# A decoder layer with PEER experts on one Trainium2 core: three steps of the query projection stage put in other places

## The chip, the cores and the metric

The kernel runs on one core of one Trainium2 chip. The metric is the device time in microseconds (us) of one execution. Its engines are TensorE (PE, with its weight loads as PEld), VectorE (DVE), ScalarE (ACT), GpSimd (POOL) and SyncE (SP); each works through its own instructions in order and waits on semaphores where the program says so. In this kernel SyncE issues the loads of the dense weights, and GpSimd issues the loads of `w_ada` and all gathers of expert rows.

## The reference

One layer on a sequence of 256 tokens, width 2048, all float32. A conditioning vector gives six vectors through `w_ada` (shift, scale, gate, twice); attention (two kinds, 8 heads each) with its output projection gives `x`; then comes the expert mixer, which is where the change lies:

```python
h2 = rmsnorm(x, norm2_g[l]) * (1.0 + sc2) + sh2
x = x + g2 * peer_ffn(h2, w_peer_q[l], peer_keys1[l], peer_keys2[l], peer_u[l], peer_v[l])
# peer_ffn, for each token and each of 8 heads:
q = h2 @ w_q                      # 8 heads x 2 halves x 128
v1, i1 = top_k(q[..., 0, :] @ keys1.T, 16); v2, i2 = top_k(q[..., 1, :] @ keys2.T, 16)
best, pos = top_k(v1[:, None] + v2[None, :], 16)      # expert = i1 * 128 + i2
gates = softmax(best)
act = gelu(u_tab[expert] @ h2)                        # one dot of 2048 for each of 16 experts
y += (gates * act) @ v_tab[expert]                    # rows of 2048
```

The result is normed once more. With 256 tokens, 8 heads and 16 experts that makes 32,768 rows of `peer_u` and as many of `peer_v`, 8 KB each.

## The kernel before

The tokens are two tiles of 128 (one per partition). The first half millisecond holds the adaLN sums, the input projection, attention and the output projection; this text is about what comes after them.

**Jobs and slots.** A job `q` is one head of one token tile, 16 jobs in all. A slot `n` (0 to 255) is one expert place of one job, `n = 16 q + k`. For a slot, one gather fetches 128 rows of `peer_u` into `u_rows` (7 buffers) and one fetches 128 rows of `peer_v` into `v_rows` (9 buffers).

**GpSimd** (L1130 to L1170) issues all gathers in one fixed order. `gather_u(n)` waits for the experts of its job, and from n = 7 on for the dot of slot n - 7, whose buffer it takes. Slot 6 takes the buffer in which an adaLN sum lay and so waits until `ada_cols(5)` has read it (`ada_columns`, L1148). The v-gathers trail: v-gather 0 stands right behind u-gather 24, v-gather 1 behind u-gather 25 and so on. v-gather 0 waits for projection `p5`, v-gather 4 for `p7`, the last, since the buffers lie in the ring of dense weights.

**VectorE** (`serve`, L1605) does for each slot `dot(n)`, a multiply of 128 x 2048 with the sum over the row written to `hidden`, and then a few pieces of `retrieve`, the top-16 search of a later job. Once per job it does `weights(q - 1)`: it waits for ScalarE's `exponent(q - 1)` and `gelu(q - 1)` and writes gate times activation into `hidden`.

**ScalarE** moves projections, scores and token rows out of PSUM, does `exponent(q)` (softmax numerator) and `gelu(q)` (which waits for the 16 dots of job q), and builds for each slot a diagonal matrix `diag` out of the weight of each token.

**TensorE** first does the eight query projections `p0` to `p7` (loop over u, L1245; for each `u` 8 steps `m` of 4 matmuls 128x256, in float32 two passes each, which the profile counts apart), the scores between them, `ada_cols(5)` (16 matmuls with one column each: the last of the six adaLN vectors), then four banks `g2b` (that vector on every partition), and then for each slot four matmuls of `diag` with the row buffer, summed in PSUM. Each pair of projections reads one 4 MB load of `w_peer_q`, in two halves. SyncE issues the halves of `w_pq3` when the ring slot has been read: the first in the middle of `u == 3`, the second at its end.

Of the kernel before, what the change touches and what calls it, by code (L numbers as in the profile page):

```python
# [62 lines left out]
def build(nc, x, c, positions, w_ada, b_ada, norm1_g, w_in, mla_q_norm_g, w_uq, mla_kv_norm_g,  # L63
# [119 lines left out]
    def take(pe, name):  # L183
        b, o = unit[name]
        if o:
            pe.wait_ge(emptied[b], o)
        return ps[:, b, :]

    def fill(ins, name):
        ins.then_inc(filled[unit[name][0]], 1)  # L190

    def full(eng, name):
        b, o = unit[name]
        eng.wait_ge(filled[b], o + 1)
        return ps[:, b, :]

    def empty(ins, name):
        ins.then_inc(emptied[unit[name][0]], 1)

    def copied(eng, name):  # L200
        b, o = unit[name]
        eng.wait_ge(emptied[b], o + 1)
# [41 lines left out]
    def loaded(eng, name, half=0):  # L244
        slot, n = item[name]
        eng.wait_ge(ring_loaded[slot][half], 16 * ring_loads[slot][half][n])
        return ring[slot]
# [46 lines left out]
    def ada_cols(part):  # L294

        nc.tensor.wait_ge(ada_steps, KC * (part + 1))
        for b in range(KC):
            ins = nc.tensor.matmul(ps[:, 7, KC * part + b:KC * part + b + 1], ada_acc[min(part, 1)][:, P * b:P * b + P],  # L298
                                   ones[:, 0:1], start=True, stop=True)
        ins.then_inc(ada_columns, 1)  # L300
# [797 lines left out]
    def used_up(eng, n):  # L1098

        eng.wait_ge(v_used[n % len(v_rows)], n // len(v_rows) + 1)  # L1100
# [3 lines left out]
    with nc.Block() as block:  # L1104
# [68 lines left out]
        def _(pe):  # L1173
# [54 lines left out]
            def score(u):  # L1228
                copied(pe, f"p{u}")
                bank = take(pe, f"sc{u}")  # L1230
                for s in range(2):
                    for t in range(TT):
                        ins = nc.tensor.matmul(bank[:, P * (2 * s + t):P * (2 * s + t) + P], pq[:, u % 2, s, P * t:P * t + P],  # L1233
                                               kT[:, H * s + u, :], start=True, stop=True)
                fill(ins, f"sc{u}")

            def token_rows(u):

                t, c = u // 4, u % 4
                bank = take(pe, f"h2_{u}")  # L1240
                for k in range(4):
                    ins = nc.tensor.transpose(bank[:, P * k:P * k + P], h2T[:, 4 * c + k, P * t:P * t + P], ident[:, :])
                fill(ins, f"h2_{u}")

            for u in range(H):  # L1245
                name, bank = f"w_pq{u // 2}", take(pe, f"p{u}")
                for m in range(PAIRS):
                    if u == 0:
                        copied(pe, f"h2T{m}")
                    if u % 2 == 0 and m % (PAIRS // 2) == 0:  # L1250
                        loaded(pe, name, m // (PAIRS // 2))
                    for k in range(2):
                        ch = 2 * m + k
                        for s in range(2):
                            lo = 512 * ch + P * (2 * (u % 2) + s)
                            ins = nc.tensor.matmul(bank[:, T * s:T * s + T], ring[item[name][0]][:, lo:lo + P], h2T[:, ch, :],  # L1256
                                                   start=(ch == 0 and s == 0), stop=(ch == KC - 1), skip_group_check=True)
                    if u % 2 and m == PAIRS // 2 - 1:
                        ins.then_inc(q_half_read, 1)
                    if u > 1 and m == 0:  # L1260
                        score(u - 1)
                    if u == 4 and m in (1, 3, 5, 7):
                        token_rows(4 + m // 2)
                    if u == 2 and m == 5:
                        ada_cols(5)
                fill(ins, f"p{u}")
                if u == 0:
                    token_rows(0)
                    score(0)
                    for k in range(1, 4):  # L1270
                        token_rows(k)
# [25 lines left out]
        def _(act):  # L1297
# [15 lines left out]
            def square(m):  # L1313
                n, t = m // 2, m % 2
                act.wait_ge(x2_part, m + 1)
                if m:
                    act.wait_ge(x2_squared, m)
                nc.scalar.activation(junk2[:, :], x2[:, t, 512 * n:512 * n + 512], ACT.Square,
                                     accum_out=st[:, 8 + 4 * t + n:9 + 4 * t + n]).then_inc(x2_squared, 1)
# [30 lines left out]
            def query(u):  # L1350
                b = full(act, f"p{u}")
                if u >= 2:
                    full(act, f"sc{u - 2}")
                empty(nc.scalar.copy(pq[:, u % 2, :, :].rearrange("p s t -> p (s t)"), b), f"p{u}")

            def scores_out(u):
                b = full(act, f"sc{u}")
                empty(nc.scalar.copy(s_all[:, :, 2 * u:2 * u + 2, :], b.rearrange("p (s t n) -> p t s n", s=2, t=TT)), f"sc{u}")

            def token_rows_out(u):  # L1360
                t, c = u // 4, u % 4
                empty(nc.scalar.copy(h2[:, t, 512 * c:512 * c + 512], full(act, f"h2_{u}")), f"h2_{u}")

            def exponent(q):
                act.wait_ge(shifted, q + 1)
                g = gate[:, q % 4, :]
                nc.scalar.activation(g, g, ACT.Exp, accum_out=gate_sum[:, q:q + 1]).then_inc(exponents, 1)

            def gelu(q):
                act.wait_ge(dots, TOPK * (q + 1))  # L1370
                d = hidden[:, q % 4, :]
                nc.scalar.activation(d, d, ACT.Gelu).then_inc(activated, 1)  # L1372
# [12 lines left out]
            for u in range(H):  # L1385
                if u == 4:
                    for k in range(4, 8):
                        token_rows_out(k)
                query(u)
                if u == 0:  # L1390
                    token_rows_out(0)
                scores_out(u)
                if u == 0:
                    for k in range(1, 4):
                        token_rows_out(k)
                if u == 4:
                    exponent(0)
                    exponent(1)
                if u == 5:
                    gelu(0)  # L1400
            for g in range(4):
                empty(nc.scalar.copy(g2b[:, 512 * g:512 * g + 512], full(act, f"g2b{g}")), f"g2b{g}")

            for q in range(QJOBS):
                if q:
                    gelu(q)
                if q == H + 1:
                    for c in range(4):
                        square(0, c)
                if q == H + 2:  # L1410
                    std(0)
                if q + 2 < QJOBS:
                    exponent(q + 2)
                act.wait_ge(weighted, q + 1)
                for k in range(TOPK):
                    n = TOPK * q + k
                    if n not in BY_VECTOR:
                        i = by_tensor.index(n)
                        if i >= len(diag):
                            used_up(act, by_tensor[i - len(diag)])  # L1420
                        nc.scalar.activation(diag[i % len(diag)][:, :], ident[:, :], ACT.Copy,  # L1421
                                             scale=hidden[:, q % 4, k:k + 1]).then_inc(diagonal, 1)
# [6 lines left out]
        def _(dve):  # L1429
# [178 lines left out]
            def serve(n):  # L1608

                q, k = divmod(n, TOPK)  # L1610
                dot(n)
                if q and k == (4 if q == 1 else 0):
                    weights(q - 1)
                if n == 6:
                    ada_finish(5)
                job, slots = (1 + k // 8, 8) if q == 0 else (q + 2, TOPK)
                if job < QJOBS:
                    for part in range(RETRIEVAL * (k % slots) // slots, RETRIEVAL * (k % slots + 1) // slots):
                        retrieve(part, job)
                if q == H + 1 and k == 1:  # L1620
                    for c in range(4):
                        take_sums(0, c)
                if q == H + 1 and k == 3:
                    for c in range(4):
                        residual(0, c)
                if q == H + 2 and k == 4:
                    variance(0)
                if q == H + 3 and k == 4:
                    dve.wait_ge(fg_loaded, 16)
                    normed(0)  # L1630
# [53 lines left out]
```

## Time and profile before

| | |
|---|---|
| median of 3 runs | 1877.13 us (1874.12 to 1878.32) |
| the profiled execution | 1878.32 us, its span 1876.6 us |
| busy, of the span | PE 78%, DVE 62%, POOL 32%, ACT 20% |
| DMA | 717.70 MB, 382 GB/s over the span |
| gathers | 512, on GpSimd's queue, 604.02 MB with the other loads there |
| granted TensorE clock, mean | 0.966 |

The span goes from the first to the last instruction of one execution. A busy share is an average over stages that have different limits: in the expert stage, from about 540 us to the end, a stretch can be bound by an engine that is not the busiest overall. So the rows below are taken by stretch and by wait. In a timeline, what stands in brackets is the time for which the engine stood idle ahead of the row, and who released it.

### The profile page before, as it was taken

How to read it: one execution, taken by the hardware profiler on the slowest of the kernel's cores; microseconds unless marked ns; L12 is line 12 of the kernel's file. 1: busy time of each engine (PE TensorE's matmuls, PEld its weight loads, DVE VectorE, ACT ScalarE, POOL GpSimd, SP SyncE). 2: the span in 40 equal slices, each digit the busy share in tenths (PEclk: the TensorE clock that was granted, in tenths of full speed). 3: DMA queues.
4: the chain of work that ended last, by engine and by line, in shares of the span. 5: the costliest groups of instructions: out<-in, count | busy, mean ns of one | idle time of the engine just before them, and what ended most of it. 6: DMA issues, size and time to landing. Idle time of an engine off the chain costs nothing.

```text
span 1876.6 us, 13765 instructions
## 1 busy us (share of the span) xinstructions
PE 1458.5 (78%) x4930; PEld 837.7 (45%) x4930; DVE 1156.9 (62%) x1541; ACT 373.8 (20%) x716; POOL 593.5 (32%) x625
## 2 busy tenths in 40 slices
PE   0289999789899897777777777777777777777776
PEld 0279987678788742323323232332322322222232
DVE  6979794668789755555555555555556556554445
ACT  1244442574401120110101011110101011010101
POOL 1001010000036565343443434344333334333331
PEclk9679999899999999999999999999999999999999
DMA  9989995728789899999999999999999999999995
GB/s 375 418 313 407 375 369 212 276 72 328 295 342 415 342 415 422 421 422 422 421 422 421 421 422 421 422 422 422 422 421 422 421 421 422 421 422 422 421 422 228
DMA packets 125328, 717.70 MB, mean 382 GB/s; under 512 B 10535, under 2 KB 14797, under 8 KB 46541
## 3 DMA queue, kind: packets, MB, share of 16 engines
q0 software_dynamic: 82976, 604.02, 77.8%
q1 hardware_dynamic: 42284, 112.81, 15.8%
q8 instruction: 39, 0.64, 0.1%
q14 instruction: 29, 0.23, 0.0%
HBM read 714.69 MB, written 2.10 MB: 382 GB/s over the span
## 4 chain that ended last, share of the span: by engine, by line
DMA 58%; PE 12%; DVE 5%; POOL 1%; issue 1%; ACT 1%; DVEq 0%; POOLq 0%
DMA u_rows<-in_peer_u,expert 51%; PE ps L1198 5%; PE ps L1256 4%; DMA v_rows<-in_peer_v,expert 4%; DVE u_rows L1570 4%; DMA ring<-in_w_peer_q 2%; PE ps L1290 2%; POOL v_rows L1139 1%; POOL u_rows L1139 1%; PE ps L298 0%; PE ps L1221 0%; PE ps L1233 0%; DVE v_rows L1651 0%; DVE x L1605 0%; PE ps L1278 0%
## 5 line engine op out<-in xcount | busy, mean ns | idle before, releaser
L1290 PE MATMUL ps<-v_rows,diag 128*128 128x512 f32 x2000 | 923.8, 607 | 282.1 <-DMA v_rows<-in_peer_v,expert 267.9
L1570 DVE SCALAR_TENSOR_TENSOR u_rows<-u_rows,h 128x2048 f32<-128x2048 f32 x256 | 586.9, 2292 | 539.7 <-DMA u_rows<-in_peer_u,expert 538.0
L1290 PEld LDWEIGHTS ps<-v_rows,diag 128*128 128x128 f32 x2000 | 364.1, 191 | 841.2 <-DMA v_rows<-in_peer_v,expert 461.0
L1139 POOL DMA_INDIRECT u_rows<-in_peer_u,expert x256 | 276.6, 1080 | 632.9 <-DVE u_rows L1570 598.7
L1139 POOL DMA_INDIRECT v_rows<-in_peer_v,expert x256 | 277.9, 1085 | 126.9 <-issue 80.5
L1421 ACT ACTIVATE diag<-ident,hidden 128x128 f32<-128x128 f32 x250 | 92.8, 397 | 721.9 <-PE ps L1290 682.7
L273 POOL DMA_DIRECT2D ada_late<-in_w_ada x64 | 34.0, 531 | 492.9 <-DVE ada_acc L287 321.5
L287 DVE SCALAR_TENSOR_TENSOR ada_acc<-ada_late,cact,ada_acc 128x2048 f32<-128x2048 f32 x60 | 140.9, 2348 | 6.7 <-DMA ada_late<-in_w_ada 5.7
L1256 PE MATMUL ps<-h2T,ring 128*128 128x256 f32 x512 | 117.3, 389 | 6.3 <-DMA ring<-in_w_peer_q 6.3
L1256 PEld LDWEIGHTS ps<-h2T,ring 128*128 128x128 f32 x512 | 99.2, 196 | 20.7 <-DMA ring<-in_w_peer_q 6.7
L556 DVE TENSOR_TENSOR ring_low<-ring,win_high 128x1024 fp32r<-128x1024 f32 (+1 forms) x64 | 74.6, 1172 | 22.8 <-ACT win_high L552 22.8
L552 ACT CAST win_high<-ring 128x1024 fp32r<-128x1024 f32 (+1 forms) x64 | 64.1, 1010 | 89.2 <-PE ps L607 32.1
L287 DVE SCALAR_TENSOR_TENSOR ada_acc<-ada_early,cact,ada_acc 128x2048 f32<-128x2048 f32 x30 | 70.5, 2351 | 10.3 <-DMA ada_early<-in_w_ada 7.7
L1372 ACT ACTIVATE hidden<-hidden 128x16 f32<-128x16 f32 x16 | 3.5, 216 | 309.7 <-DVE u_rows L1570 309.6
L433 PE MATMUL ps<-ident,xs 128*128 128x128 f32 x32 | 7.0, 409 | 55.3 <-ACT xs L455 45.5
L298 PE MATMUL ps<-ones,ada_acc 128*128 128x1 f32 x192 | 31.5, 298 | 20.7 <-DVE ada_acc L287 20.7
L1198 PE MATMUL ps<-wo_high,mix_high_part 128*128 128x512 f32 x128 | 41.6, 407 | 3.3 <-DVE ring_low L556 3.3
L607 PE MATMUL ps<-hT_high,win_high 128*128 128x256 f32 x256 | 42.2, 288 | 0.1
L607 PE MATMUL ps<-hT_low,win_high 128*128 128x256 f32 x256 | 42.0, 287 | 0.0
L552 ACT CAST wo_high<-ring 128x1024 fp32r<-128x1024 f32 x32 | 33.7, 1053 | 40.7 <-PE ps L1198 40.7
L601 PE MATMUL ps<-win_high,hT_high 128*128 128x512 f32 (+1 forms) x128 | 37.9, 378 | 4.8 <-DVE ring_low L556 4.8
L298 PEld LDWEIGHTS ps<-ones,ada_acc 128*128 128x128 f32 x192 | 31.9, 261 | 21.0 <-DVE ada_acc L287 20.8
(253 smaller groups left out, 1234.3 us busy)
## 6 DMA issues: line engine op xcount, KB each, us to landing
ada_late<-in_w_ada POOLq DMA_DIRECT2D x64, 1024.0 KB, 7.9
ada_early<-in_w_ada SPq DMA_DIRECT2D x32, 1024.0 KB, 17.7
ring<-in_w_in SPq DMA_DIRECT2D x14, 2048.0 KB, 17.7
ring<-in_w_o SPq DMA_DIRECT2D x8, 2048.0 KB, 17.2
ring<-in_w_peer_q SPq DMA_DIRECT2D x8, 2048.0 KB, 17.1
u_rows<-in_peer_u,expert POOLq DMA_INDIRECT x256, 32.2
v_rows<-in_peer_v,expert POOLq DMA_INDIRECT x256, 33.5
ring<-in_w_uq SPq DMA_DIRECT2D x1, 3072.0 KB, 16.8
```

What stands on the lines that cost most here:

```text
L287: nc.vector.scalar_tensor_tensor(out=a, in0=buf[:, :], scalar=cact[:, kc:kc + 1], in1=a, op0=ALU.mult, op1=ALU.add).then_inc(ada_steps, 1)
L298: ins = nc.tensor.matmul(ps[:, 7, KC * part + b:KC * part + b + 1], ada_acc[min(part, 1)][:, P * b:P * b + P], ones[:, 0:1], start=True, s ...
L552: nc.scalar.copy(self.high, self.whole).then_inc(made, 1)
L556: nc.vector.tensor_tensor(self.low, self.whole, self.high.bitcast(F32), ALU.subtract).then_inc(done, 1)
L601: ins = nc.tensor.matmul(banks[t][:, 0:width], h[:, ch, P * t:P * t + P], w.of(part, k), start=first, stop=last)
L607: ins = nc.tensor.matmul(banks[b // 2][:, T * (b % 2):T * (b % 2) + T], w.of(part, k, P * b, P), h[:, ch, :], start=first and b % 2 == 0, ...
L1139: nc.gpsimd.indirect_dma_start(buf[:, :], None, table, bass.IndirectOffsetOnAxis(ap=expert[:, q, k:k + 1], axis=0)).then_inc(done, 16)
L1198: ins = nc.tensor.matmul(banks[t], mixed[:, h, P * t:P * t + P], w.of(part, k), start=first, stop=last)
L1256: ins = nc.tensor.matmul(bank[:, T * s:T * s + T], ring[item[name][0]][:, lo:lo + P], h2T[:, ch, :], start=(ch == 0 and s == 0), stop=(ch ...
L1290: ins = nc.tensor.matmul(ps[:, c, :], diag[i % len(diag)][:, :], buf[:, 512 * c:512 * c + 512], start=(n % HALF_SLOTS == 0), stop=last)
L1421: nc.scalar.activation(diag[i % len(diag)][:, :], ident[:, :], ACT.Copy, scale=hidden[:, q % 4, k:k + 1]).then_inc(diagonal, 1)
L1570: nc.vector.scalar_tensor_tensor(out=buf[:, :], in0=buf[:, :], scalar=1.0, in1=h2[:, q // H, :], op0=ALU.mult, op1=ALU.mult, accum_out=hid ...
```

## The change

Three edits. `ada_cols(5)` goes from step 5 of `u == 2` to step 4 of `u == 3`. `exponent(0)`, `exponent(1)` and `gelu(0)` go from the loop over the projections on ScalarE to behind the copies of `g2b`. On VectorE `weights(0)` goes from behind the dot of slot 20 to behind the dot of slot 16, where the `weights` of every other job stand.

```diff
--- before.py
+++ after.py
@@ -1261,7 +1261,7 @@
                         score(u - 1)
                     if u == 4 and m in (1, 3, 5, 7):
                         token_rows(4 + m // 2)
-                    if u == 2 and m == 5:
+                    if u == 3 and m == 4:
                         ada_cols(5)
                 fill(ins, f"p{u}")
                 if u == 0:
@@ -1393,17 +1393,13 @@
                 if u == 0:
                     for k in range(1, 4):
                         token_rows_out(k)
-                if u == 4:
-                    exponent(0)
-                    exponent(1)
-                if u == 5:
-                    gelu(0)
             for g in range(4):
                 empty(nc.scalar.copy(g2b[:, 512 * g:512 * g + 512], full(act, f"g2b{g}")), f"g2b{g}")
 
+            exponent(0)
+            exponent(1)
             for q in range(QJOBS):
-                if q:
-                    gelu(q)
+                gelu(q)
                 if q == H + 1:
                     for c in range(4):
                         square(0, c)
@@ -1609,7 +1605,7 @@
 
                 q, k = divmod(n, TOPK)
                 dot(n)
-                if q and k == (4 if q == 1 else 0):
+                if k == 0 and q:
                     weights(q - 1)
                 if n == 6:
                     ada_finish(5)
```

On TensorE, at the projections `u == 2` and `u == 3` (`ring_50` and `ring_49` are the two slots of the weight ring; L1256 is a projection, L1233 a score, L298 `ada_cols`):

```order
 L1256 MATMUL ps<-h2T,ring_50 128x256 x4
 L1233 MATMUL ps<-kT,pq 128x128 x4
-L1256 MATMUL ps<-h2T,ring_50 128x256 x20
+L1256 MATMUL ps<-h2T,ring_50 128x256 x32
+L1233 MATMUL ps<-kT,pq 128x128 x4
+L1256 MATMUL ps<-h2T,ring_50 128x256 x16
 L298 MATMUL ps<-ones,ada_acc_75 128x1 x16
 L1256 MATMUL ps<-h2T,ring_50 128x256 x12
-L1233 MATMUL ps<-kT,pq 128x128 x4
-L1256 MATMUL ps<-h2T,ring_50 128x256 x28
 L1256 MATMUL ps<-h2T,ring_49 128x256 x4
 L1233 MATMUL ps<-kT,pq 128x128 x4
```

`ada_cols(5)` now stands 28 matmuls and one score later, with 12 matmuls left before the projections of the other ring slot begin.

On ScalarE, before, from behind the copies of projection 4 on (L1354 moves a projection, L1358 scores, L1367 is `exponent`, L1372 `gelu`, L1402 a copy of `g2b`):

```order
L1367 ACT_TABLE_LOAD
L1367 ACTIVATE gate,gate_sum<-gate 128x16 x2
L1354 COPY pq<-ps 128x512
L1358 COPY s_all<-ps 128x2x256
L1372 ACT_TABLE_LOAD
L1372 ACTIVATE hidden<-hidden 128x16
L1354 COPY pq<-ps 128x512
L1358 COPY s_all<-ps 128x2x256
L1354 COPY pq<-ps 128x512
L1358 COPY s_all<-ps 128x2x256
L1402 COPY g2b<-ps 128x512 x4
```

And now, from the same place (L1397 is what was L1402):

```order
L1354 COPY pq<-ps 128x512
L1358 COPY s_all<-ps 128x2x256
L1354 COPY pq<-ps 128x512
L1358 COPY s_all<-ps 128x2x256
L1354 COPY pq<-ps 128x512
L1358 COPY s_all<-ps 128x2x256
L1397 COPY g2b<-ps 128x512 x4
L1367 ACT_TABLE_LOAD
L1367 ACTIVATE gate,gate_sum<-gate 128x16 x2
L1372 ACT_TABLE_LOAD
L1372 ACTIVATE hidden<-hidden 128x16
```

The exponents and the first gelu have moved behind projection 7 and behind all four copies.

On VectorE, before, from the dot of slot 16 to the first weights (L1570 is a dot, L1575 and L1578 are `weights`, the others retrieval):

```order
L1570 SCALAR_TENSOR_TENSOR u_rows_120,hidden<-u_rows_120,h_115 128x2048
L1502 MAX tk_v<-s_all 128x8
L1570 SCALAR_TENSOR_TENSOR u_rows_121,hidden<-u_rows_121,h_115 128x2048
L1504 MAX_INDEX tk_i<-tk_v,s_all 128x8
L1505 MATCH_REPLACE rest<-tk_v,s_all 128x128
L1570 SCALAR_TENSOR_TENSOR u_rows_122,hidden<-u_rows_122,h_115 128x2048
L1507 MAX tk_v<-rest 128x8
L1570 SCALAR_TENSOR_TENSOR u_rows_123,hidden<-u_rows_123,h_115 128x2048
L1509 MAX_INDEX tk_i<-tk_v,rest 128x8
L1570 SCALAR_TENSOR_TENSOR u_rows_124,hidden<-u_rows_124,h_115 128x2048
L1575 RECIPROCAL gate_sum<-gate_sum 128x1
L1578 SCALAR_TENSOR_TENSOR hidden<-hidden,gate_sum,gate 128x16
```

And now, from the same dot (L1566 is a dot, L1571 and L1574 are `weights`):

```order
L1566 SCALAR_TENSOR_TENSOR u_rows_120,hidden<-u_rows_120,h_115 128x2048
L1571 RECIPROCAL gate_sum<-gate_sum 128x1
L1574 SCALAR_TENSOR_TENSOR hidden<-hidden,gate_sum,gate 128x16
L1498 MAX tk_v<-s_all 128x8
L1566 SCALAR_TENSOR_TENSOR u_rows_121,hidden<-u_rows_121,h_115 128x2048
L1500 MAX_INDEX tk_i<-tk_v,s_all 128x8
L1501 MATCH_REPLACE rest<-tk_v,s_all 128x128
```

The two instructions of `weights(0)` have passed four dots and the retrieval between them.

## Rows read from the trace of the kernel before

**Rows 1.** The page, the chain that ended last, share of the span by engine.

```profile
DMA 58%; PE 12%; DVE 5%; POOL 1%; issue 1%; ACT 1%; DVEq 0%; POOLq 0%
```

**Rows 2.** Four stretches: start:end, length, each engine's busy us, granted clock, DMA share, GB/s.

```profile
600.00:644.00 44.00, 37.68 (x179) 32.87 (x178) 40.08 (x69) 6.53 (x13) 24.89 (x14) 0.92 1.02 417
644.00:652.00 8.00, 7.68 (x36) 6.42 (x34) 3.88 (x7) 0.28 (x1) 0.05 (x1) 1.00 0.20 79
652.00:660.00 8.00, 5.01 (x41) 4.84 (x42) 0.00 (x0) 5.49 (x12) 6.17 (x7) 1.00 0.78 264
660.00:1840.00 1180.00, 903.55 (x1957) 356.06 (x1956) 628.97 (x917) 139.46 (x327) 480.40 (x470) 0.99 1.01 422
```

**Rows 3.** The timeline of GpSimd: start us, length us, engine line op, count, [idle before <-releaser].

```profile
562.33 0.94 POOL L1139 DMA_INDIRECT u_rows<-in_peer_u,expert  x1 [6.26 <-PE ps L298]
...
614.85 0.94 POOL L1139 DMA_INDIRECT u_rows<-in_peer_u,expert  x1 [1.66 <-DVE u_rows L1570]
...
651.95 0.94 POOL L1139 DMA_INDIRECT v_rows<-in_peer_v,expert  x1 [14.66 <-PE ps L1256]
```

**Rows 4.** Tiles u_rows and v_rows on GpSimd, 540 to 640 us: count, first and last start.

```profile
L1139 POOL DMA_INDIRECT u_rows<-in_peer_u,expert x29: 939/2115/3048, 542.9 to 634.9; - x29
...
L1139 POOL DMA_INDIRECT v_rows<-in_peer_v,expert x4: 2194/2344/2596, 616.1 to 632.2; - x4
```

**Rows 5.** The timeline of TensorE, projections and ada columns.

```profile
548.86 8.80 PE L1256 MATMUL ps<-h2T,ring 128*128 128x256 f32 x40
557.50 4.56 PE L298 MATMUL ps<-ones,ada_acc 128*128 128x1 f32 x32
561.92 7.83 PE L1256 MATMUL ps<-h2T,ring 128*128 128x256 f32 x24
...
616.36 5.35 PE L1256 MATMUL ps<-h2T,ring 128*128 128x256 f32 x24
628.02 10.68 PE L1256 MATMUL ps<-h2T,ring 128*128 128x256 f32 x40 [6.32 <-DMA ring<-in_w_peer_q]
```

**Rows 6.** Tile ring on SyncE's queue, 560 to 580 and 580 to 600 us.

```profile
L242 SPq DMA_DIRECT2D ring<-in_w_peer_q x1: 368/368/368, 575.9 to 575.9; - x1
...
DMA to landing us min/median/max: 28.9/28.9/28.9
...
L242 SPq DMA_DIRECT2D ring<-in_w_peer_q x1: 368/368/368, 582.8 to 582.8; - x1
...
DMA to landing us min/median/max: 45.2/45.2/45.2
```

**Rows 7.** The timeline of ScalarE, activations and the last copy of g2b.

```profile
602.45 1.28 ACT L1367 ACT_TABLE_LOAD   x1
...
604.07 0.19 ACT L1367 ACTIVATION_READ_ACCUMULATOR gate<-gate 128x1 f32 x1
...
617.16 1.28 ACT L1372 ACT_TABLE_LOAD   x1
618.45 0.22 ACT L1372 ACTIVATE hidden<-hidden 128x16 f32<-128x16 f32 x1
...
657.12 0.59 ACT L1402 COPY g2b<-ps 128x512 f32<-128x512 f32 x1 [0.31 <-issue]
```

**Rows 8.** The timeline of VectorE: dot 6, dot 16, weights(0).

```profile
573.73 2.29 DVE L1570 SCALAR_TENSOR_TENSOR u_rows<-u_rows,h 128x2048 f32<-128x2048 f32 x1
...
609.69 2.28 DVE L1570 SCALAR_TENSOR_TENSOR u_rows<-u_rows,h 128x2048 f32<-128x2048 f32 x1
...
622.83 0.23 DVE L1578 SCALAR_TENSOR_TENSOR hidden<-hidden,gate_sum,gate 128x16 f32<-128x16 f32 x1
```

**Rows 9.** Timelines of ScalarE, VectorE and GpSimd at the second weights.

```profile
689.18 0.22 ACT L1372 ACTIVATE hidden<-hidden 128x16 f32<-128x16 f32 x1
...
689.51 0.24 DVE L1578 SCALAR_TENSOR_TENSOR hidden<-hidden,gate_sum,gate 128x16 f32<-128x16 f32 x1 [11.15 <-ACT hidden L1372]
...
692.60 0.94 POOL L1139 DMA_INDIRECT u_rows<-in_peer_u,expert  x1 [7.29 <-DVE u_rows L1570]
```

## The prediction

> **What bounds the kernel now.** I read the chain of waits first. Of the span, 58% lies on DMA and 12% on TensorE, VectorE has 5% [rows 1]. Then the busy table by stretches: from 660 to 1840 us the DMA engines are full (share 1.01, 422 GB/s), while TensorE is busy 904 of 1180 us and VectorE 629 [rows 2]. This stretch fetches rows of `peer_u` and `peer_v`, 512 gathers in all, each 128 rows of 2048 floats, 1.049 MB. At 422 GB/s one costs 2.485 us. Nothing an engine saves there shortens the kernel; what counts is how many gathers are done when it begins, and when it begins.
>
> Just ahead of it the DMA runs dry: 79 GB/s from 644 to 652 and 264 GB/s from 652 to 660, against 417 from 600 to 644 [rows 2]. GpSimd, which issues all gathers in one order, says why: after its u-gather at 634.9 it waits 14.66 us for TensorE, and issues v-gather 4 at 651.95 [rows 3]. That wait is for `p7`, the last query projection (v buffer 4 lies in the weight ring that `p7` reads). By then 29 u-gathers (n = 0 to 28) and 4 v-gathers had been issued [rows 4]. TensorE reaches `p7` late in part because it stands idle for 6.32 us before 628.02, until a half of `w_pq3` lands; its 40 passes behind that take 10.68 us where 40 in full flow take 8.80 [rows 5].
>
> **Part 1, the last ada columns.** `ada_cols(5)`, 32 passes, moves back by 56 passes of projection (28 matmuls of two passes) and one score. It took 4.42 us (557.50 to 561.92), and the 24 passes behind it 7.83 instead of 24 × 0.22 = 5.3 [rows 5]. Both go with it, still ahead of `p3` (24 passes follow it in `u == 3`), so `p3`, and every PE instruction after it, keeps its time: 0. Two things hang on its end. GpSimd waits for it before u-gather 6, issued at 562.33 [rows 3]: 56 passes at 0.216 (548.86 to 557.50 is 40 of them) and a score of 0.9 later makes 13.0 us, so 575.3. Without the cover below that would starve VectorE, which does dot 6 at 573.73 [rows 8]. And the first half of `w_pq3`, which waits for the middle of `u == 3`, is issued 4.4 + 2.5 = 6.9 us earlier than 575.9, at 569.0, while no gather is on its way.
>
> **The w_pq3 load.** Its first half was issued at 575.9 and took 28.9 us, to 604.8; the second was issued at 582.8 and took 45.2, to 628.0, so 23.2 us after the first [rows 6]. With the first half out of the way (2.1 MB, 5 us at the full rate), the second needs about 23 us from 582.8 and lands near 606. TensorE wants it where it stopped, 616.36 + 5.35 = 621.7 [rows 5]. The idle 6.32 us goes, and the slow passes behind it (10.68 − 8.80 = 1.88): `p7` is ready 8.2 us earlier, near 643.5. By itself a gain; bounds: 0 (the load still late) and 8.2. I take 8.2, since the margin is 15 us, and in the middle of this time gathers stop altogether (next part).
>
> **Part 2, the activations and the first weights.** ScalarE did `exponent(0)`, `exponent(1)` at 602.45 to 604.26 and `gelu(0)` at 617.16 to 618.67 [rows 7]; they are now behind the four copies of `g2b`, thus behind `p7`, the last score and `g2b`'s matmuls. VectorE did `weights(0)` at 622.83, after dot 20 [rows 8]; it now stands after dot 16, whose dot started at 609.69 [rows 8]. Dot 16 can be later by up to the 13.0 us of part 1, so VectorE is at `weights(0)` between 612 and 625, and waits there for an exponent and a gelu that ScalarE hasn't reached. VectorE's queue is in order: dot 17 and all retrieval stand behind it.
>
> Who waits for that: u-gather n waits for dot n − 7, so 23 is the last (dot 16). u-gather 24, at 614.85 before [rows 3], is stuck, and with it v-gather 0, which is issued behind it. So only 24 gathers are made ahead of the stall, where before 33 were: 9 fewer. The last 7 need at most 7 × 2.49 = 17.4 us, so they have landed by 643 even at the latest, and the DMA then stands still; the 13 us of part 1 lie inside that.
>
> When does it end? The last `g2b` copy ended at 657.12 + 0.59 = 657.71 [rows 7]; less 8.2, 649.5. Then the exponents (602.45 to 604.26, with table load: 1.81) and the gelu (617.16 to 618.67, with table load: 1.51) [rows 7] end at 652.8. From the end of a gelu over the weights, one piece of retrieval and one dot to the next u-gather the trace shows the same sequence once: gelu ends 689.18 + 0.22, GpSimd issues at 692.60, 3.20 us [rows 9]. So u-gather 24 is issued at 656.0, against v-gather 4 at 651.95 before: 4.1 us later, with 9 gathers more to do.
>
> On the table loads a rule of the Trainium skill speaks for more. The rows have the gelu start 1.29 us behind the start of its load, straight behind it [rows 7]. The page "ScalarE: Activation LUTs", section "What ACT_TABLE_LOAD costs", says a switch also pays about 1.38 us of drain, 2.66 us in all. By that the two switches would hold 2.8 us more and the sum come out that much larger; the trace shows no such gap, and the measured rows decide.
>
> **Refill.** Before, the DMA started with 264 GB/s over 8 us, 3.0 us lost, with GpSimd issuing one gather each 1.25 us. Now two are issued like that, then two for each dot with its retrieval (about 3 us), which is less than the 5 us they need. No row shows it exactly: bounds 0 and 3 (that loss once more); I take 0.5, near the row's own behaviour.
>
> **Sum.** 9 × 2.485 = 22.4, plus 4.1, plus 0.5: 27.0 us slower. The profiled execution took 1878.32 us (span 1876.6), so 1905.3; the median of the runs is 1.2 us less, so 1904. Its own range, with the refill's bounds, the 1.9 us of slow passes kept or not, and 1.5 us of scatter in the runs, is 1901 to 1909. The long stretch after it cannot absorb any of it, as its DMA share is 1.01; the tail behind the last gather only moves.
>
> **Rivals.**
> *A, TensorE keeps its wait.* If the second half of `w_pq3` still lands after 628, `p7` stays at 651.7 and all is 8.2 us later: 1912. For it: gathers hog the engines while both are out (45.2 us for 2 MB). Against: the first half is gone before gather 6, and gathers stop near 625. Chance 0.07.
> *B, a drain at each table switch* as the page has it: GpSimd would restart 2.8 us later: 1907. Against: rows 7. Chance 0.04.
> *C, the restart is shallow.* Before, VectorE waited at the next `weights` until 689.51 and GpSimd sat idle 7.29 us before 692.60 [rows 9], with the DMA full from a deep queue. If the queue is shallow then, those 7.3 us are lost: 1911. Against: two gathers per dot are issued at 3 us a pair against 5 us of work, and v-gather 7, which the gelu hangs on, comes at the same time as u-gather 31. Chance 0.05.
> *D, not slower.* The mechanism is the gather queue again, with the other sign: if gather 6, 13 us late, holds VectorE back so that it comes to `weights(0)` only after the gelu at 652.8, nothing is stuck, the 33 gathers are made, and only the earlier `p7` is left: up to 8.2 us faster, 1869. It decides at 652.8, and dot 16 ends by 625 even if the full 13.0 are passed on; it would need 41 us of delay against 13. Break-even in another way: the stall would have to end 26 us earlier. Chance 0.03.
>
> **How the numbers follow.** The forecast has 0.81, A 0.07, B 0.04, C 0.05, D 0.03. The range 1900 to 1912 holds the forecast's own range, B and C, and most of A. A change under 0.2% (3.8 us) can't be told from none; that needs most of 27 us to be missing, for which I keep 0.01 of D's share. Slower 0.97, same 0.01, faster 0.02.
>
> **What would show it.** In the profile after: GpSimd issues u-gather 6 near 575, u-gather 24 near 656 with some 30 us of idle time in front of it; VectorE waits some 30 us at `hidden` or `gate_sum` for ScalarE; the DMA share is near 0 from about 643 to 656 and low from 635; TensorE has no wait for the ring; the full stretch begins near 660 and lasts 22 us longer. Wrong would be: an idle TensorE at the ring load (A), the DMA share under 0.9 anywhere between 670 and 720 (C), or no wait on VectorE at all (D).

## The result, and the profile after

| | before | after |
|---|---|---|
| median of 4 runs | 1877.72 us | 1909.05 us (1907.04 to 1913.46) |
| ratio | | 1.0168, 95% interval 1.0139 to 1.0198 |
| profiled execution, its span | 1878.32, 1876.6 us | 1906.7, 1904.7 us |

The changed kernel is slower by 26 to 37 us; the forecast was 1904 within 1900 to 1912. The two profiled executions lie 28.4 us apart, and the account below is made against these.

The page's chain that ended last, against [rows 1]: the DMA's share is 2 points smaller and GpSimd's (POOL) 2 points larger.

```profile
DMA 56%; PE 13%; DVE 5%; POOL 3%; issue 2%; ACT 1%; DVEq 0%; POOLq 0%
```

The busy table by stretches (start:end, length, busy us of PE, PEld, DVE, ACT, POOL, the granted clock, DMA share, GB/s), against [rows 2]:

```profile
600.00:630.00 30.00, 30.00 (x149) 26.64 (x148) 18.54 (x33) 2.34 (x4) 11.73 (x7) 1.00 0.98 403
630.00:656.00 26.00, 17.70 (x104) 15.71 (x103) 3.56 (x10) 11.01 (x25) 0.46 (x1) 0.90 0.00 1
656.00:660.00 4.00, 0.00 (x0) 0.00 (x0) 3.93 (x4) 0.30 (x2) 3.39 (x3) 0.50 0.71 250
660.00:700.00 40.00, 28.46 (x55) 11.51 (x56) 31.52 (x50) 2.41 (x6) 34.51 (x19) 0.86 0.99 386
700.00:1860.00 1160.00, 877.96 (x1887) 343.47 (x1886) 619.91 (x905) 135.31 (x315) 468.74 (x463) 0.99 1.01 422
```

For 26 us nothing is transferred. The DMA ran dry near 629; the prediction had 643 as the latest time for that and named it as the sign. Running dry earlier costs nothing more, as no further gather had been issued. The full stretch has the same rate as before; it only starts later and has more to do. New to me is the row of 660 to 700: its DMA share of 0.99 looks full, but 386 GB/s are 9% less than 422.

GpSimd's timeline, against [rows 3]: gathers u 6, 23, 24 and v 0, u 25.

```profile
575.68 0.94 POOL L1139 DMA_INDIRECT u_rows<-in_peer_u,expert  x1 [18.01 <-PE ps L298]
...
619.72 0.94 POOL L1139 DMA_INDIRECT u_rows<-in_peer_u,expert  x1 [3.44 <-DVE u_rows L1566]
655.54 0.94 POOL L1139 DMA_INDIRECT u_rows<-in_peer_u,expert  x1 [34.88 <-DVE u_rows L1566]
656.78 2.20 POOL L1139 DMA_INDIRECT v_rows<-in_peer_v,expert  x1 [0.30 <-issue]
659.28 2.28 POOL L1139 DMA_INDIRECT u_rows<-in_peer_u,expert  x1 [0.30 <-issue]
```

It stands still for 34.88 us between u-gather 23 and 24, put down to VectorE's dot. The tile `u_rows` on GpSimd from 540 to 650 us, against [rows 4], has 24 gathers, and `v_rows` none:

```profile
L1139 POOL DMA_INDIRECT u_rows<-in_peer_u,expert x24: 932/1010/3037, 544.5 to 619.7; - x24
```

VectorE's timeline, against [rows 8]: dot 16, then both instructions of `weights(0)`.

```profile
617.16 2.28 DVE L1566 SCALAR_TENSOR_TENSOR u_rows<-u_rows,h 128x2048 f32<-128x2048 f32 x1
...
650.65 0.16 DVE L1571 RECIPROCAL gate_sum<-gate_sum 128x1 f32<-128x1 f32 x1 [31.20 <-ACT gate L1367]
...
652.46 0.23 DVE L1574 SCALAR_TENSOR_TENSOR hidden<-hidden,gate_sum,gate 128x16 f32<-128x16 f32 x1 [1.64 <-ACT hidden L1372]
```

The wait before them is 31.20 us for the exponent and 1.64 for the gelu. ScalarE's timeline, against [rows 7], has both behind the last copy of `g2b`:

```profile
648.41 0.58 ACT L1397 COPY g2b<-ps 128x512 f32<-128x512 f32 x1 [0.31 <-PE ps L1278]
649.02 1.28 ACT L1367 ACT_TABLE_LOAD   x1
...
650.84 1.28 ACT L1372 ACT_TABLE_LOAD   x1
652.13 0.21 ACT L1372 ACTIVATE hidden<-hidden 128x16 f32<-128x16 f32 x1
```

TensorE's timeline, against [rows 5]: there is no idle time at the ring any more, and where 40 passes took 10.68 us, 64 in one piece take 13.98.

```profile
571.78 3.63 PE L298 MATMUL ps<-ones,ada_acc 128*128 128x1 f32 x32
575.27 8.84 PE L1256 MATMUL ps<-h2T,ring 128*128 128x256 f32 x32
...
616.01 13.98 PE L1256 MATMUL ps<-h2T,ring 128*128 128x256 f32 x64
```

### The profile page after: what moved, and what is told of

Its sections match the earlier page's. It is cut to its first block, busy times and chain, and to the rows that moved or that the text cites. A ratio compares the mean times of both kernels' runs of the same rounds, so it can differ in the third digit from the quotient of the medians.

```text
span 1904.7 us, 13765 instructions
## 1 busy us (share of the span) xinstructions
PE 1463.5 (77%) x4930; PEld 835.3 (44%) x4930; DVE 1157.0 (61%) x1541; ACT 373.8 (20%) x716; POOL 592.1 (31%) x625
## 4 chain that ended last, share of the span: by engine, by line
DMA 56%; PE 13%; DVE 5%; POOL 3%; issue 2%; ACT 1%; DVEq 0%; POOLq 0%
DMA u_rows<-in_peer_u,expert 52%; PE ps L1256 6%; PE ps L1198 5%; DMA v_rows<-in_peer_v,expert 4%; DVE u_rows L1566 4%; POOL v_rows L1139 2%; POOL u_rows L1139 1%; PE ps L1233 0%; PE ps L298 0%; PE ps L1221 0%; DVE v_rows L1647 0%; DVE x L1601 0%; PE ps L1290 0%; PE ps L1278 0%; PE ps L1179 0%
## 5 line engine op out<-in xcount | busy, mean ns | idle before, releaser
L1290 PE MATMUL ps<-v_rows,diag 128*128 128x512 f32 x2000 | 933.6, 612 | 309.2 <-DMA v_rows<-in_peer_v,expert 297.6
L1566 DVE SCALAR_TENSOR_TENSOR u_rows<-u_rows,h 128x2048 f32<-128x2048 f32 x256 | 586.8, 2292 | 543.5 <-DMA u_rows<-in_peer_u,expert 542.0
L1256 PE MATMUL ps<-h2T,ring 128*128 128x256 f32 x512 | 114.4, 383 | 0.0
L1256 PEld LDWEIGHTS ps<-h2T,ring 128*128 128x128 f32 x512 | 97.4, 192 | 13.1
L552 ACT CAST win_high<-ring 128x1024 fp32r<-128x1024 f32 (+1 forms) x64 | 64.2, 1009 | 90.7 <-PE ps L601 31.3
L1372 ACT ACTIVATE hidden<-hidden 128x16 f32<-128x16 f32 x16 | 3.5, 216 | 309.6 <-DVE u_rows L1566 309.5
L298 PE MATMUL ps<-ones,ada_acc 128*128 128x1 f32 x192 | 29.0, 285 | 20.7 <-DVE ada_acc L287 20.7
L1198 PE MATMUL ps<-wo_high,mix_low_part 128*128 128x512 f32 x128 | 41.2, 404 | 0.0
```

Source lines behind the costliest of these rows:

```text
L552: nc.scalar.copy(self.high, self.whole).then_inc(made, 1)
L1198: ins = nc.tensor.matmul(banks[t], mixed[:, h, P * t:P * t + P], w.of(part, k), start=first, stop=last)
L1290: ins = nc.tensor.matmul(ps[:, c, :], diag[i % len(diag)][:, :], buf[:, 512 * c:512 * c + 512], start=(n % HALF_SLOTS == 0), stop=last)
L1566: nc.vector.scalar_tensor_tensor(out=buf[:, :], in0=buf[:, :], scalar=1.0, in1=h2[:, q // H, :], op0=ALU.mult, op1=ALU.mult, accum_out=hid ...
```

## The experiments

Each ratio is against the kernel before, run on the same chip as the experiment (medians of before: 1878.42 for e1 to e4, 1877.85 for e5 to e7; 1877.72 in the table above). The theory: the loss is the number of gathers that are not yet issued when GpSimd comes to stand still, times 2.485 us, and the delay of its restart. The rival: the late activations or the late ada columns cost by themselves.

**e1: the stall four dots later.** (against the changed kernel)

```diff
-                if k == 0 and q:
+                if q and k == (4 if q == 1 else 0):
```

> The changed kernel with one edit undone: weights(0) again behind dot 20. Theory (gathers missing at the stall): VectorE makes 4 more dots before it waits, so GpSimd issues 8 more gathers (u 24 to 27, v 0 to 3), worth 8 x 2.485 = 19.9 us; the end of the stall stays. About 1889 us, within 4. Rival (the loss comes from ScalarE's later activations or from the late ada columns themselves, wherever VectorE waits): no change against the changed kernel, 1909.

Measured: 1886.48 us, ratio 1.0040 (1.0024 to 1.0056). GpSimd's timeline has the missing eight gathers ahead of a shorter stall:

```profile
632.17 0.94 POOL L1139 DMA_INDIRECT v_rows<-in_peer_v,expert  x1 [0.30 <-issue]
652.49 0.94 POOL L1139 DMA_INDIRECT u_rows<-in_peer_u,expert  x1 [19.38 <-DVE u_rows L1566]
```

ScalarE and TensorE do the same as in the changed kernel, but all of it 3.05 us earlier: in this execution the first projection, which stands ahead of everything that was edited, began at 511.88 instead of 514.93. 22.6 us of the 31.3 between the medians are gone. The eight gathers account for 19.9 of them; the earlier start is of the size of the rest, and no run tells whether it belongs to the edit. Once the activations are late, the place of one wait, by four dots, holds most of the loss.

**e2: only the ada columns moved.**

```diff
-                    if u == 2 and m == 5:
+                    if u == 3 and m == 4:
                         ada_cols(5)
```

> The kernel before with only ada_cols(5) moved. Theory: gather 6 comes 13 us later, but the idle DMA time at 644 to 655 takes that up, and p7 is ready 8.2 us earlier; DMA idle before the full stretch shrinks from about 9.5 us to about 4. 1872 us, within 4, so a little faster than before. Rival (gather 6 late starves VectorE and this is a part of the loss of the whole change): 1885 to 1891.

Measured: 1874.15 us, ratio 0.9978 (0.9961 to 0.9996), a small gain. The two stretches in which it loses and wins; the first is 396 GB/s before, the others [rows 2]:

```profile
540.00:580.00 40.00, 40.00 (x202) 35.57 (x201) 29.87 (x53) 2.35 (x4) 14.44 (x10) 0.96 0.90 338
...
644.00:652.00 8.00, 5.37 (x33) 4.17 (x32) 6.20 (x12) 6.60 (x16) 6.78 (x5) 0.84 1.02 425
652.00:660.00 8.00, 8.00 (x18) 3.46 (x18) 4.74 (x5) 0.81 (x2) 6.48 (x6) 0.94 1.01 419
```

It loses 58 × 40 / 422 = 5.5 us while gather 6 is late, and wins 6.6 and 2.9 from 644 to 660; net 4.0. The medians lie 4.3 apart, the two profiled executions 2.6. The halves of `w_pq3` landed 7.9 and 29.1 us after their issue at 569.2 and 581.3, against 28.9 and 45.2 [rows 6]. e1 differs from e2 only in the late activations and is 12.3 us slower in the median: with `weights(0)` in its old place, behind dot 20, they do cost.

**e3: the activations and the weights moved, the ada columns not.**

```diff
-                    if u == 3 and m == 4:
+                    if u == 2 and m == 5:
                         ada_cols(5)
```

(against the changed kernel)

> The changed kernel with ada_cols(5) back at its old place. Theory: the stall of VectorE begins 9 us earlier but at the same dot, so the same 9 gathers are missing; the second half of w_pq3 lands a little earlier than 628 since gathers stop near 625, TensorE waits some 4 us and all comes 4 to 7 us later than in the changed kernel: 1914 us, within 3. Rival (the ada move causes a part of the loss): under 1900.

Measured: 1914.79 us, ratio 1.0195 (1.0173 to 1.0216). TensorE and GpSimd, from their timelines:

```profile
627.62 11.69 PE L1256 MATMUL ps<-h2T,ring 128*128 128x256 f32 x40 [4.31 <-DMA ring<-in_w_peer_q]
```

```profile
664.87 0.94 POOL L1139 DMA_INDIRECT u_rows<-in_peer_u,expert  x1 [49.57 <-DVE u_rows L1566]
```

The wait for the ring is 4.31 us, as expected some 4, and the restart comes at 664.87 instead of 655.54, 9.3 us later. The profiled executions lie 9.5 us apart, the medians 5.7. So the ada edit gains here too. The 49.57 us of idle time are 14.7 more than 34.88 and cost only these 9.3, as the same 24 gathers were made: the length of a wait does not tell its price.

**e4: only `weights(0)` moved, the activations in place.**

```diff
-                if q and k == (4 if q == 1 else 0):
+                if k == 0 and q:
```

(against the kernel before)

> The kernel before with only weights(0) moved behind dot 16; the activations keep their place. Theory: dot 16 ends at 612 and the gelu at 618.7, a stall of about 7 us at a time when p7 is 33 us away and GpSimd has to wait for it anyway: 1878 us, within 3, no change. Rival (the place of weights(0) costs by itself, one stall of VectorE being one stall of the gathers): 7 us, 1885.

Measured: 1875.88 us, ratio 0.9990 (0.9972 to 1.0008): no change. Its VectorE does wait, 5.41 us:

```profile
619.39 0.23 DVE L1578 SCALAR_TENSOR_TENSOR hidden<-hidden,gate_sum,gate 128x16 f32<-128x16 f32 x1 [5.41 <-ACT hidden L1372]
```

and GpSimd's wait for `p7` shrinks from 14.66 to 7.41 us. A stall that ends inside slack further down costs nothing. Alone, the early weights cost nothing here, and the late activations cost 12.3 us (e1 against e2); the other 22.6 (e1 against the changed kernel) need both, as the one makes VectorE come early and the other makes it wait long.

**e5: the stall eight dots later.** As e1, with `8` for `4`.

> The changed kernel with weights(0) behind dot 24, later than in either kernel. Theory (the price is the number of gathers missing when GpSimd stands still): VectorE comes there near 641, GpSimd is by then held by p7 and not by VectorE, and goes on at 643; no gather is missing for long, so the time is that of the late ada columns alone, 1874 us, within 4. Rival 1 (5 us for each dot, without end): 1867. Rival 2 (the late exponent and gelu cost by themselves once dot 20 is reached): 1886, as with dot 20.

Measured: 1875.50 us, ratio 0.9985 (0.9969 to 1.0001), the time of e2. VectorE still waits 13.30 + 1.64 us, and from 600 us on the DMA is full all along:

```profile
644.00:652.00 8.00, 1.12 (x11) 0.93 (x9) 0.16 (x1) 3.41 (x8) 3.76 (x4) 0.89 1.02 423
652.00:660.00 8.00, 4.93 (x6) 2.19 (x7) 6.61 (x12) 4.98 (x13) 2.81 (x2) 0.50 1.01 422
```

One step of the expectation was wrong: GpSimd did not wait for `p7`. It issued v-gather 4 at 640.41 after 0.30 us, went on to v-gather 7 at 647.89, and then stood for 8.06 us behind VectorE, with 40 gathers made and the queue deep enough to cover that. So the late activations cost nothing if VectorE comes late enough (rival 2 falls), and the dose has an end (rival 1 falls): 0, 4 and 8 more dots give 1909.05, 1886.48 and 1875.50.

**e6: short dots during the refill.** Dots 17 to 31 read a quarter of their columns; that part of the computation is left out.

```diff
+                w = D // 4 if 17 <= n < 32 else D
-                nc.vector.scalar_tensor_tensor(out=buf[:, :], in0=buf[:, :], scalar=1.0, in1=h2[:, q // H, :], op0=ALU.mult,
+                nc.vector.scalar_tensor_tensor(out=buf[:, 0:w], in0=buf[:, 0:w], scalar=1.0, in1=h2[:, q // H, 0:w], op0=ALU.mult,
```

> The changed kernel, with dots 17 to 31 done on the first 512 of 2048 columns only, so part of the computation is left out there. Question: why the DMA moves 373 to 407 GB/s instead of 422 from 660 to 700 after the stall (3.3 us lost). Theory (GpSimd's gather instruction can't get done while a dot of VectorE runs, so one gather goes out per dot, each 2.6 to 2.7 us, more than the 2.485 us of its transfer): with short dots GpSimd's gathers take 0.94 us for the most part, DMA stays at 415 or more from 662 to 700, and the time is about 3 us under the changed kernel's, 1905. Rival (the instruction is slow because the queue fills up): gathers still take 2.2 to 2.9 us with 370 to 390 GB/s and the time is unchanged.

Measured: 1903.51 us, ratio 1.0120 (1.0085 to 1.0155), against 1.0168 (1.0139 to 1.0198) of the changed kernel: some 5 us less between the medians, with intervals that overlap, and 2.2 us between the profiled executions. The v-gathers on GpSimd from 656 to 680 us (shortest, median, longest ns), first of the changed kernel, then of e6; and e6's stretch from 660 to 700:

```profile
L1139 POOL DMA_INDIRECT v_rows<-in_peer_v,expert x5: 2197/2346/2600, 656.8 to 677.9; - x5
```

```profile
L1139 POOL DMA_INDIRECT v_rows<-in_peer_v,expert x9: 937/941/1435, 657.1 to 678.0; - x9
```

```profile
660.00:700.00 40.00, 28.27 (x57) 11.31 (x58) 12.81 (x44) 2.81 (x7) 25.66 (x27) 0.88 1.01 414
```

With 2293 ns dots back to back a gather takes 2346 ns, with 693 ns dots 941, and the DMA has 414 GB/s in place of 386. The timelines show what holds it. In the changed kernel, from 640 to 1860 us, 36 gathers start while a dot runs, and each of them ends 0.80 to 0.82 us after that dot does; of the 452 others 425 take 0.94 us. The two dots here end at 658.16 and 660.75, and the gathers that started during them, shown further up, end at 658.98 and 661.56:

```profile
655.87 2.29 DVE L1566 SCALAR_TENSOR_TENSOR u_rows<-u_rows,h 128x2048 f32<-128x2048 f32 x1
...
658.46 2.29 DVE L1566 SCALAR_TENSOR_TENSOR u_rows<-u_rows,h 128x2048 f32<-128x2048 f32 x1
```

In e6, up to 680 us, four gathers start during a dot. Two start 0.1 us before its end and take 0.94; the others start soon after it begins, at 658.37 and 667.52, take 1.38 and 1.44 us and end 0.82 after it. The first of these, with its dot:

```profile
658.24 0.69 DVE L1567 SCALAR_TENSOR_TENSOR u_rows<-u_rows,h 128x512 f32<-128x512 f32 x1
```

```profile
658.37 1.38 POOL L1139 DMA_INDIRECT u_rows<-in_peer_u,expert  x1 [0.30 <-issue]
```

So a gather that starts during a dot is held until the dot is over, with dots of 2.29 and of 0.69 us alike, and in the refill the next gather starts during the next dot. At 2.7 us a dot with its retrieval that is less than one gather per 2.485 us, and the refill is not full. The rival, a queue that fills up and slows the instruction, falls: in e6 the queue was fuller, as a v-gather of that window landed 23.0 us after its issue in the median against 6.9 in the changed kernel. By the rates of the stretches the refill loses 2.8 us in e6 and 5.5 in the changed kernel; with a restart 0.3 us later that makes 2.4 less, close to the 2.2 between the profiled executions. More than that is not shown.

**e7: the same rule with the other sign.** The kernel before, v-gathers 28 slots behind instead of 24 up to slot 35.

```diff
-                while given < n + 1 - TOPK - max(0, min(8, 10 - n // TOPK)):
+                while given < n + 1 - TOPK - (12 if n < 36 else max(0, min(8, 10 - n // TOPK))):
```

> The kernel before with one edit on GpSimd: v-gathers trail by 28 slots instead of 24 up to slot 35, so that v-gather 4, which waits for p7, stands behind u-gather 32 instead of 28. Theory (the price is gathers made by the time of the stall): 4 more gathers fit in ahead of p7, 9.9 us, and fill the idle DMA time of 644 to 655: 1869 us, within 3, the same stall with the opposite sign. Rival (VectorE, one dot each 2.7 us, is what limits them, or the lost time comes back in the next weights): 1874 to 1878.

Measured: 1870.24 us, ratio 0.9952 (0.9934 to 0.9970), so 7.6 us less than before, where four gathers more are worth 9.9. GpSimd's wait for `p7` is down from 14.66 to 2.92 us, and the hole in the DMA is filled:

```profile
651.90 0.94 POOL L1139 DMA_INDIRECT v_rows<-in_peer_v,expert  x1 [2.92 <-PE ps L1256]
```

```profile
644.00:652.00 8.00, 7.63 (x36) 6.37 (x34) 7.75 (x14) 0.34 (x1) 4.78 (x3) 1.00 1.00 416
652.00:660.00 8.00, 5.06 (x41) 4.84 (x42) 6.15 (x8) 5.50 (x12) 6.78 (x5) 1.00 1.02 422
```

This version is faster than both kernels, by an edit of one number, though its VectorE waits 29.59 us at the second `weights` where it waited 11.15 [rows 9]. That wait hides behind a full queue.

## Why the prediction was right, and where it was off

**The mechanism was right.** VectorE stands at `weights(0)` behind dot 16, GpSimd behind u-gather 24, and the DMA is dry. e1, e4 and e5 show that the full loss takes both the early weights and the late activations, and that the price follows the gathers made.

**The sum, term by term, of the profiled executions.**

| term | forecast | measured |
|---|---|---|
| 9 gathers × 2.485 | 22.4 | 22.4 (33 and 24 counted) |
| restart of GpSimd | 4.1 (651.95 to 656.0) | 3.6 (to 655.54) |
| refill | 0.5 | 2.5 |
| sum | 27.0 | 28.5, against 28.4 |

The measured refill: of 655.54 to 660 the DMA misses 0.46 + 4 × (1 − 250/422) = 2.1 us, of 660 to 700 another 40 × (1 − 386/422) = 3.4, together 5.5; before it was 3.0.

**The restart came out near for a partly lucky reason.** Its 0.5 us less than forecast is the difference of two things that the sum did not have: this execution began its first projection 1.4 us later than the one before (514.93 against 513.55), and TensorE gained 1.9 us more on the way than the 8.2 forecast (below). What follows the last `g2b` copy came out as forecast: from there to the end of the gelu 3.35 us, and from the gelu to u-gather 24 3.20, the value of [rows 9].

**The refill is the term that was mis-sized.** "Two are issued like that, then two for each dot" was wrong: while dots run back to back it is one gather per dot. The pace was wrong too, 2.7 us for a dot with its retrieval and not about 3. The bounds (0 and 3) held the refill; the value taken lay near the wrong end. Rows of before had the sign: four v-gathers of 2194 to 2596 ns during dense dots [rows 4], against 0.94 in the rows where VectorE was idle [rows 3].

**The ada columns.** u-gather 6 came at 575.68 (forecast 575.3), the ring wait went, and the last `g2b` copy began 8.7 us earlier (648.41 against 657.12; forecast 8.2), though the first projection began 1.4 us later in this execution, so 10.1 were gained in between. To the 8.2 comes what I had put at no change: 3.49 us from the start of the columns to the next projection (571.78 to 575.27) against 4.42, and 1.8 us over full pace behind them (8.84 for 32 passes at 0.22) against 2.5, together 1.6; some 0.3 are left. What differs is the granted clock: 0.66 from 560 to 570 before, 0.83 from 570 to 580 after. No run here tells why, and it stays open. The second half of `w_pq3` was forecast to need about 23 us; in e2, which has the same order of TensorE here, it needed 29.1, and the margin of 15 us held that.

**Rivals.** A (TensorE keeps its wait) falls by the row at 616.01. B (a drain at each table switch) falls: the gelu starts 1.29 us after its load starts, at 652.13, and the load starts 0.02 us after the end of the exponents. C put its price at the wrong place: VectorE's second `weights` waited only 0.95 us, and the queue was shallow for another reason. Its sign, a DMA share under 0.9, did not come either: in stretches of 5 us from 670 to 720 the share was never under 0.92, while the rate fell to 334 GB/s. D (VectorE comes late enough) did not happen, since it came at 619, and e5 comes near it: behind eight more dots VectorE still waits, but with 40 gathers made nothing is lost by it.

**The medians** differ by 31.3 us and the profiled executions by 28.4; the interval, 26 to 37, covers both, and no run shows a cause for the rest. The first projection begins, in the nine profiled executions, anywhere from 511.62 (e5) to 516.87 us (e6), though no edit stands ahead of it; so a comparison of two single executions carries a few microseconds from before the changed stage, and the 28.5 against 28.4 of the table is closer than it can be trusted. The prediction's own range, 1901 to 1909, is also added up wrong by 1 us: its parts give 1902 to 1910. The measured median of 1909.05 lies near the upper end of that, 5 us above the forecast.

## What to carry to other kernels

Where a long stretch is held by a full DMA queue, count what has been issued when its issuer stands still, and when it goes on; the length of a wait alone does not tell its price. VectorE waits 31.20 us at a `weights` in the changed kernel (1909.05 us) and 29.59 in the fastest one, e7 (1870.24). A wait moved a few instructions up an in-order queue can cost more than the work it waits for, if another engine's queue hangs on what now stands behind it. Moving an activation later is free only as long as its reader comes later too, as in e5.

## What the runs showed of the hardware

A gather issued by GpSimd takes 0.94 us when VectorE is idle, and 2.2 to 2.9 in the refill of the changed kernel, where VectorE runs 2.29 us products of two SBUF operands one after another; it then ends 0.8 us after the end of a product (e6). The page "SBUF — State Buffer" of the Trainium skill, section "SBUF: two separate sides", has the rule: VectorE and GpSimd share one pair of ports, held for a whole instruction, by VectorE also with two SBUF inputs if GpSimd's operation reads SBUF. The trace agrees in that a gather which starts during a product is held until it ends, by 2.29 us products and by 0.69 us ones; that it is the ports that hold it, no run here shows. The DMA share of 0.99 in that stretch hid the loss; only GB/s showed it.
